# Expert blocks fed by column copies from on-chip transposed rows, addressed by token numbers in registers

## The reference

```
h = rmsnorm(x);  x += concat(sliding_window_gqa(h), multiscale_pool(h)) @ w_out
h = rmsnorm(x);  x += cross_attention(h, rmsnorm(mem)) @ xo_w          # 256 memory tokens
h = rmsnorm(x)                                                        # 512 x 2048
g_logits = h @ rg_w + rg_b                 # 4 groups; top 1
e_logits = h @ re_w[g] + re_b[g]           # 8 experts in the group; top 2, softmax of the two
for each of the 32 experts e:              # its tokens, in blocks
    y = (silu(xb @ w_gate[e]) * (xb @ w_up[e])) @ w_down[e]    # 2048 -> 512 -> 2048
    x[tokens] += gate * y
```

## Time and profile before

| | |
|---|---|
| three runs | 1660.6, 1664.76 (median), 1665.17 us |
| profiled execution | 1662.8 us, its span 1661.0 us |
| mean granted TensorE clock | 0.983 |
| PE busy | 1555.2 us (94%) |
| PE weight load busy | 887.2 us (53%) |
| DVE busy | 637.2 us (38%) |
| ACT busy | 358.0 us (22%) |
| POOL busy | 166.2 us (10%) |
| moved by DMA | 484.47 MB, mean 292 GB/s |
| chain that ended last | PE 70%, DMA 18%, DVE 7% |

### The profile page before, as it was taken

The page is one execution under the profiler, slowest core; times in us unless marked ns, Lnnn a source line. Parts: engine busy times, 40 slices in busy tenths (PEclk is TensorE's granted clock), DMA queues, the critical chain, the costliest instruction groups (busy, mean ns, idle before and its releaser), DMA issues.

```text
span 1661.0 us, 18188 instructions
## 1 busy us (share of the span) xinstructions
PE 1555.2 (94%) x7236; PEld 887.2 (53%) x7236; DVE 637.2 (38%) x783; ACT 358.0 (22%) x640; POOL 166.2 (10%) x235
## 2 busy tenths in 40 slices
PE   7999999999999999899999899889889899999997
PEld 6787777768887567733433334334334334334353
DVE  5755656652223432513322323223323223313224
ACT  6422334342223244211110011011011011101011
POOL 4470045510000000100000000000000000000000
PEclk9999999999999999999999999999999999999999
DMA  8332222353215031899999999999999999999997
GB/s 305 103 102 76 82 72 77 120 167 101 102 51 203 1 127 48 347 407 429 397 429 428 428 426 429 428 428 404 429 428 427 411 416 427 428 426 425 427 423 287
DMA packets 91773, 484.47 MB, mean 292 GB/s; under 512 B 6066, under 2 KB 44108, under 8 KB 64204
## 3 DMA queue, kind: packets, MB, share of 16 engines
q1 hardware_dynamic: 88232, 470.84, 70.0%
q0 software_dynamic: 3392, 12.92, 2.3%
q10 hardware_dynamic: 100, 0.03, 0.0%
HBM read 484.81 MB, written 8.39 MB: 297 GB/s over the span
## 4 chain that ended last, share of the span: by engine, by line
PE 70%; DMA 18%; DVE 7%; issue 2%; ACT 2%; SPq 1%; POOL 0%; DVEq 0%; POOLq 0%; ACTq 0%
PE ps L2248 22%; DMA weight_ring<-in_expert_w_up_dram 16%; PE ps L1954 10%; PE ps L1828 10%; PE ps L2274 7%; PE ps L2209 5%; PE ps L2007 3%; DVE residual L1633 3%; DMA weight_ring<-in_xkv_w_dram 1%; PE ps L1790 1%; PE ps L2070 1%; PE ps L2338 1%; PE ps L2095 1%; ACT weight_ring L898 1%; PE ps L1883 1%
## 5 line engine op out<-in xcount | busy, mean ns | idle before, releaser
L2248 PE MATMUL ps<-weight_ring,transposed_acts 128*64 128x512 f32 x2000 | 471.8, 611 | 52.6 <-DMA weight_ring<-in_expert_w_up_dram 51.3
L2248 PEld LDWEIGHTS ps<-weight_ring,transposed_acts 128*64 128x64 f32 x2000 | 158.5, 141 | 358.2 <-issue 279.5
L1633 DVE TENSOR_TENSOR residual<-ps,residual 128x1024 f32<-128x1024 f32 x128 | 150.8, 1219 | 265.3 <-PE ps L2209 264.8
L2274 PE MATMUL ps<-weight_ring,transposed_acts 128*64 128x512 f32 x960 | 212.6, 595 | 4.9 <-DVE transposed_acts L1643 4.8
L1649 DVE SCALAR_TENSOR_TENSOR y_low<-ps,proj_buffer,y_high 64x1024 fp32r<-64x1024 f32 x60 | 77.0, 1283 | 198.0 <-ACT y_high L1090 197.1
L2274 PEld LDWEIGHTS ps<-weight_ring,transposed_acts 128*64 128x64 f32 x960 | 71.9, 137 | 128.1 <-issue 125.7
L1090 ACT ACTIVATE y_high<-ps,proj_buffer 64x1024 fp32r<-64x1024 f32 x60 | 66.6, 1109 | 286.7 <-PE ps L2274 286.0
L1079 ACT ACTIVATE transposed_acts<-ps 128x512 f32<-128x512 f32 x32 | 19.1, 598 | 475.3 <-PE ps L2248 475.3
L1828 PE MATMUL ps<-mix_high,w_in_high 128*128 128x512 f32 x288 | 117.3, 407 | 1.4 <-issue 1.4
L1828 PE MATMUL ps<-normed_low,w_in_high 128*128 128x512 f32 x288 | 112.3, 390 | 0.0
L1828 PE MATMUL ps<-mix_high,w_in_low 128*128 128x512 f32 x288 | 112.3, 390 | 0.0
(11 more groups left out here) (315 smaller groups left out, 1895.3 us busy)
## 6 DMA issues: line engine op xcount, KB each, us to landing
weight_ring<-in_expert_w_down_dram SPq DMA_DIRECT2D x63, 2048.0 KB, 15.1
weight_ring<-in_expert_w_gate_dram SPq DMA_DIRECT2D x61, 2048.0 KB, 16.0
weight_ring<-in_expert_w_up_dram SPq DMA_DIRECT2D x60, 2048.0 KB, 20.3
weight_ring<-in_w_in_dram SPq DMA_DIRECT2D x18, 1024.0 KB, 5.6
weight_ring<-in_w_out_dram SPq DMA_DIRECT2D x16, 1024.0 KB, 5.0
weight_ring<-in_xkv_w_dram SPq DMA_DIRECT2D x8, 1024.0 KB, 7.6
residual<-in_x_dram SPq DMA_DIRECT2D x8, 1024.0 KB, 12.8
weight_ring<-in_xq_w_dram SPq DMA_DIRECT2D x4, 1024.0 KB, 9.8
```

Source lines behind the costliest of these rows:

```text
L1633: v.tensor_tensor(part, ps[:, bank:bank + 2, :].rearrange("p b n -> p (b n)"), part, ALU.add).then_inc(signal, 1)
L2248: ins = mm(ps[side * SLOTS:(side + 1) * SLOTS, 0, :], xsT[:, k, par * SLOTS:(par + 1) * SLOTS], gate_up_weights(e, u, kk), start=(k == 0), ...
L2274: ins = mm(ps[half, 4 + n % 2, :], act_t[:, f * SLOTS:(f + 1) * SLOTS], w[:, n * 512:(n + 1) * 512], start=(f == 0), stop=(f == KF - 1), s ...
```

## The change

The normalised rows are no longer stored and no longer gathered. H stays whole on chip, and the columns of a block are copied out of it.

- **Removed:** the buffer `normed_rows`, its four stores and ScalarE's and GpSimd's waits for them; the 17 gathers and the clearing of `hs[:, 0]` before the first; `turn_rows` and `turn_evac`; the extra buffers of expert 3, whose units 0 and 1 are now loaded through the ring like all others. SP's loop begins at expert 2.
- **Moved:** `xsT` to PB columns 0 to 2047, and the buffers `gu`, `sil`, `act_t`, `last_act_t` from H to PB. The load of `xo_w` signals on four of the ring's semaphores. The token ramp now comes behind the first column copies. `turn_gu` of a pair's second block stands before a wait for `part_added`.
- **Copies:** `copy_columns` loads 32 token numbers into registers of the engine, each with a check that it lies in 0 to 511, and issues 32 copies of 128 x 16 elements, column `where[j]` of H to a column of `xsT`, twice a block. For blocks 0 and 1 ScalarE copies slots 0 to 31 and GpSimd slots 32 to 63; in the loop GpSimd copies all 64 of each block. The copies of block b >= 2 wait until `gu_copied` has reached b - 1, that is until block b - 2 no longer needs its half of `xsT`. `gate_up` waits for the copies in place of `turn_evac`.
- **Ids:** a table `ids` (48 blocks x 64 slots, integers) is made by eight more matmuls (with the operands of the token product exchanged) and one VectorE step, and stored by GpSimd in DRAM (`block_ids`, 12 KB). The loop fetches a pair's 512 bytes with a DMA into `first_row` on one partition. For the first pair there is a path of its own: right after `ranks` VectorE makes one-hot matrices for experts 0 and 1 (`rank1`, `first_onehot`), TensorE multiplies them with the rounded token numbers (four matmuls), and VectorE writes `first_row` (`first_ids`), ahead of the rest of the router's chain. Empty slots are clamped to token 511 by `ALU.min`.
- **Logits:** the 36 router columns are now the stationary operand, and 128 tokens move; even chunks of features go to the lower half of the array, odd ones to the upper, into bank 5, which VectorE clears first. VectorE copies the result out (`logits_out`), and one more matmul with a constant matrix (`fold`) adds the two halves and turns them back to tokens on partitions (`fold_logits`). `keep_busy` counts change from 14 to 4 and 16 around the first pair's token product, and from 8 to 6 before block 0.

```diff
-            for t in range(NT):
-                pool.wait_ge(rows_ready, 4 * t + 4)
-                pool.dma_start(hn_dram[t * P:(t + 1) * P, :], hs[:, t % 2, :]).then_inc(hn_stored[t % 2], 16)
-            pool.wait_ge(hn_stored[0], 32)
-            pool.wait_ge(h_turned, 4 * 13)
-            g.memset(hs[:, 0, :], 0.0).then_inc(xs_clear, 1)
-            def gather(pair):
...
-                g.indirect_dma_start(out=xs, out_offset=None, in_=hn_dram,
-                                     in_offset=bass.IndirectOffsetOnAxis(ap=cols[:, 0:1], axis=0),
-                                     bounds_check=S - 1, oob_is_err=False).then_inc(gathered, 16)
+            def copy_columns(tokens, par, first, done, free=None):
+
+                for at in range(first, SLOTS, 32):
+                    _, where = nc.values_load_multi_w_load_instructions(
+                        tokens[:, at:at + 32], engines=(mybir.EngineType.Pool,), min_val=0, max_val=S - 1)
+                    if at == 0:
+                        pool.wait_ge(gu_copied, free)
+                    for j in range(32):
+                        ins = g.tensor_copy(xsT[:, :, par * SLOTS + at + j], H[:, :, ds(where[j], 1)].rearrange("p k n -> p (k n)"))
+                ins.then_inc(done, 1)
+
+            pool.wait_ge(first_ids, 1)
+            pool.wait_ge(h_turned, 56)
+            for par in range(2):
+                copy_columns(first_row[0:1, par * SLOTS:(par + 1) * SLOTS], par, 32, first_rows[par])
             pool.wait_ge(table_ready, 1)
             g.iota(tramp, pattern=[[1, S]], base=0, channel_multiplier=0,
                    allow_small_or_imprecise_dtypes=True).then_inc(tramp_ready, 1)
-            gather(1)
-            with pool.Fori(2, NE // 2 + 1) as it:
-                gather(it)
+            pool.wait_ge(ids_ready, 1)
+            pool.dma_start(ids_dram.rearrange("j (e s) -> (j e) s", e=2), ids[:, :]).then_inc(ids_stored, 16)
...
+            def pair_columns(it):
+                pool.dma_start(first_row[0:1, :], ids_dram[ds(it, 1), :]).then_inc(pair_ids_in, 16)
+                landed_ids = pool.to_reg(it * 16)
+                pool.wait_ge(pair_ids_in, landed_ids)
+                block_columns(it * 2, 0)
+                block_columns(it * 2 + 1, 1)
+
+            with pool.Fori(1, NE // 2) as it:
+                pair_columns(it)
@@ scalar
+            act.wait_ge(first_ids, 1)
+            act.wait_ge(h_turned, 56)
+            act.wait_ge(hT_ready, 56)
+            for par in range(2):
+                _, where = nc.values_load_multi_w_load_instructions(
+                    first_row[0:1, par * SLOTS:par * SLOTS + 32], engines=(mybir.EngineType.Activation,), min_val=0, max_val=S - 1)
+                for j in range(32):
+                    ins = a.activation(xsT[:, :, par * SLOTS + j], H[:, :, ds(where[j], 1)].rearrange("p k n -> p (k n)"), ACT.Copy)
+                ins.then_inc(first_rows[par], 1)
@@ sync
-            sp.wait_ge(hn_stored[1], 32)
-            sp.wait_ge(h_turned, 56)
-            load_extra(0)
-            sp.wait_ge(logits_done, 1)
-            load_extra(1)
-            load_extra(2)
             sp.wait_ge(table_ready, 1)
-            sp.wait_ge(gathered, 16)
...
-            load_extra(3)
...
-            with sp.Fori(EXTRA + 2, NE - 2) as b:
+            with sp.Fori(2, NE - 2) as b:
@@ vector
+            link(v.scalar_tensor_tensor(out=r["rank1"], in0=R[:, :, 0:2], scalar=1.0, in1=M_r[:, 0:NT, 0:2].bitcast(F32),
+                                        op0=ALU.add, op1=ALU.mult))
+            v.scalar_tensor_tensor(out=P_r[:, :, :], in0=wide(io[:, 0:SLOTS].unsqueeze(1), P, 2 * NT, SLOTS), scalar=1.0,
+                                   in1=wide(r["rank1"].rearrange("p t e -> p (t e)").unsqueeze(2), P, 2 * NT, SLOTS),
+                                   op0=ALU.add, op1=ALU.is_equal).then_inc(first_onehot, 1)
...
+            dve.wait_ge(first_tokens, 1)
+            v.tensor_scalar(first_row, ps[0:1, 4, 0:2 * SLOTS], float(ABSENT), float(S - 1), ALU.add, ALU.min).then_inc(first_ids, 1)
...
+            v.tensor_scalar(ids[:, :], ps[0:NBLK, 6, 0:SLOTS], float(ABSENT), float(S - 1), ALU.add, ALU.min).then_inc(ids_ready, 1)
...
-            def turn_evac(pair):
@@ tensor
-                    for k in range(4 * b, 4 * b + 4):
-                        ins = mm(ps[:, 4, t * NCOL:(t + 1) * NCOL], H[:, k, t * P:(t + 1) * P], wr[:, k, :],
-                                 start=(m == 0 and k == 4 * b), stop=(m == 3 and k == 4 * b + 3), skip_group_check=True)
+                    for j in range(4):
+                        k, side = 4 * b + j, j % 2
+                        ins = mm(ps[side * SLOTS:side * SLOTS + NCOL, 5, t * P:(t + 1) * P], wr[:, k, :], H[:, k, t * P:(t + 1) * P],
+                                 start=(m == 0 and j < 2), stop=(m == 3 and j >= 2), skip_group_check=True)
+            def fold_logits(t):
+                pe.wait_ge(halves_out, t + 1)
+                return mm(ps[:, 4, t * NCOL:(t + 1) * NCOL], LT[t % 2], fold[:, :], start=True, stop=True)
...
-            def turn_rows(pair, between=None):
...
             def gate_up(b, par, place=None, between=None):
-                if par == 0:
-                    pe.wait_ge(xsT_ready, b * 2 + 4)
+                if isinstance(b, int) and b < 2:
+                    pe.wait_ge(first_rows[b], 2)
+                else:
+                    pe.wait_ge(block_rows, b - 1)
```

More of the change, by code:

```diff
@@ L56 @@
 NSLOT = 12
-EXTRA = 3
 NA = 4
@@ L386, in hybrid_block @@
             loads_before.append(sum(1 for m in range(n) if early[m][0] == s))
-        early_loads = [sum(1 for e in early if e[0] == s) for s in range(NSLOT)]
+        before_xo = [sum(1 for e in early if e[0] == s) for s in range(NSLOT)]
+        early_loads = [n + (s in (4, 6, 8, 10)) for s, n in enumerate(before_xo)]
         def wait_past(eng, semaphore, value):
@@ L603, in _ @@
                             pattern=[[-1, P]], channel_multiplier=1).then_inc(consts, 1)
+            pool.wait_ge(consts, 2)
+            link(g.tensor_tensor(fold[:, :], ident[:, 0:NCOL], ident[:, SLOTS:SLOTS + NCOL], ALU.add))
             link(g.memset(blk[:, :], 0.0))
@@ L2148, in _ @@
             ins.then_inc(ranks, 1)
-            keep_busy(14)
+            keep_busy(4)
+            pe.wait_ge(first_onehot, 1)
+            pair_onehot = P_r[:, :, :].rearrange("p (t e) s -> p t (e s)", e=2)
+            for t in range(NT):
+                ins = mm(ps[0:2, 4, 0:2 * SLOTS], tok_r[:, t, :], pair_onehot[:, t, :], start=(t == 0), stop=(t == NT - 1))
+            ins.then_inc(first_tokens, 1)
+            keep_busy(16)
             pe.wait_ge(slot_onehot, 1)
@@ L2161, in _ @@
             ins.then_inc(gates_done, 1)
-            def turn_rows(pair, between=None):
-                rows = pair * 16 + 16
-                if not isinstance(pair, int):
-                    rows = pe.to_reg(rows)
-                pe.wait_ge(gathered, rows)
-                for q in range(4):
-                    if q == 2 and between is not None:
-                        between()
-                    for k in range(4 * q, 4 * q + 4):
-                        ins = turn(ps[:, TURN_BANKS[q], (k % 4) * P:(k % 4 + 1) * P],
-                                   hs[:, 0, k * P:(k + 1) * P], ident[:, :])
-                    ins.then_inc(xs_turned, 1)
             def expert_landed(b, u):
                 s = unit_slot(u)
-                if isinstance(b, int) and b == EXTRA and u < 2:
-                    pe.wait_ge(extra_in, 16 * 5)
-                elif isinstance(b, int) and b == 0 and u == 3:
+                if isinstance(b, int) and b == 0 and u == 3:
                     pe.wait_ge(first_up_in, 16 * 3)
```

135 lines of the change are left out of this document (61 added, 74 removed).

## The result

The changed kernel takes 1741.88 us (median of 4 runs, 1741.45 to 1744.3) beside 1663.91 us before: ratio 1.0477, 95% interval 1.0462 to 1.0492. It is 4.8% slower. Forecast were 1650 us and a range up to 1735; the forecast was wrong, and even the range misses by 7 us. The profiled execution is one of 1744.3 us with a span of 1742.5.

The account below looks back on a forecast made before the run. The weight stream was taken to set the pace, 59.4 us a pair. Gathers -20, extra buffers +9.9, start -2 and tail -0.4 gave -12.5 from 1662.8: 1650 us (chance 0.60, own range 1642 to 1658), overall range 1641 to 1735.

Parts of the forecast that it names:

- the loop: GpSimd's copies, loads and ids' DMA for a pair: 57.6 us, hidden under 59.4; 0.4 us saved in the tail.
- A second step: In the loop: GpSimd's work for a pair costs no time if it fits under the weight stream's 59.4 us.
- Rival A: GpSimd's loop, 15 pairs, sets the pace; each microsecond above 59.9 a pair costs 14.5; 1691 to 1865 us; chance 0.31.
- with one far jump a pair: Case of GpSimd setting the pace: a jump to unfetched code in its loop, a pair of 62 us, 1691 us.
- Gathers: In the weight stream: 7.9 MB of gathered rows go, 20 us saved (18.6 to 23.2).
- Extra buffers: Before block 0: four pieces of expert 3 (4.19 MB) now fall into the weight stream, 9.9 us lost.
- Start: First two blocks: ids at 689.0, first product at 702.8, 2 us earlier (bounds 6 earlier, 8 later).
- Sum without GpSimd: Whole kernel, GpSimd's loop taken as hidden: -20 + 9.9 - 2 - 0.4 = -12.5 us.
- What would show it: Signs of being wrong: TensorE waiting for copies every pair, DMA share under 0.97, pairs above 60, slow loads, first product after 708.

Follow-up runs that it names:

- e1: Changed kernel with GpSimd's 15 pairs written out instead of looped, so without the backward jump: 1682.13 us, ratio 1.0122.
- e3: Changed kernel with the ids of all 32 blocks fetched once, in one DMA before the loop; the far jump stays: 1700.43 us, ratio 1.0227.
- e4: Changed kernel without GpSimd's check of each id, run twice: 1642.05 us (ratio 0.9874), the second time 1640.7 us (0.9866).
- e2: Changed kernel with GpSimd's load-and-copy body standing once, in an inner loop over halves and blocks: 1754.62 us, ratio 1.0557.
- e5: Changed kernel without GpSimd's checks and with its 15 pairs written out instead of looped: 1661.85 us, ratio 0.9999.
- f9: Changed kernel with GpSimd's 15 pairs written out and its checks kept only on every second load of ids: 1669.83 us, ratio 1.0042.
- g13: Kernel before, with four checked loads of 32 zeros on GpSimd behind each gather, pairs written out: 1673.58 us, ratio 1.0071.
- g14: Kernel before, with four checked loads of 32 zeros on GpSimd behind each gather, in loops: 1664.51 us, ratio 1.0008.
- e6: Changed kernel with all ids fetched once and GpSimd's body standing once in an inner loop, checks kept: 1668.98 us, ratio 1.0042.
- t10: Changed kernel without GpSimd's checks, with TensorE's loop over 13 pairs written out: 1643.53 us, ratio 0.988.

## Why the prediction was wrong

**The step that failed** is the loop: "I take 6. A pair: 57.6 us. It fits, by two microseconds." GpSimd's pair takes 65.0. Term by term:

| us | forecast | measured |
|---|---|---|
| load of 32 ids | 3.6 | 2.03 |
| check, each | 0.12 | 0.23 |
| copy, each | 0.17 | 0.15 |
| half block | 12.9 | 13.2 |
| ids' DMA, issue to ids on chip | 6 | 5.8 |
| far jump | 0 | 5.2 |
| pair | 57.6 | 65.0 |

In a half the load came out 1.6 us under the forecast and the copies 0.6, the 32 checks 3.5 over it, and 1.0 of that is hidden (below): 0.3 remain, 1.3 in a pair. What decided was the jump, priced at nothing in the sum although it stood in rival A, with the earlier trace rows beside it (4.33 us for TensorE's). e1 shows its price: without it 59.5 us a pair and 60 us less. The rest (65.0 - 4 x 13.2 - 5.8 - 5.2 = 1.2) are small steps. The measured half, 13.2, is a little less than its pieces (2.03 + 32 x 0.23 + 4.8 = 14.2), because the sequencer is 1 us ahead of the copies when it begins the next load. That the sum passed the limit by so little is why the chance of 0.60 was too high.

**A second step** behind it wouldn't have held either: "That is hidden if it fits under 59.4 us". In e3 the pair takes 58.9 us and fits, and the time is 1700 us, not 1650. Theory F's kind of loss, weights that come slower where GpSimd fetches code, stands in no term of the forecast.

**Rival A** came true, in the case "with one far jump a pair". It was given 62 us a pair and 1691; at 65.0 its own formula gives 1662.8 + 5.1 x 14.5 - 2.4 = 1734. The measured profiled time is 1744. The formula left out the end. From block 2 to block 30 are 14 pairs that grow by 5.0 us, 70; and block 31's rows come 26.1 us behind block 30's, so that the stretch from block 30 to the end grows from 69.7 to 79.4, 10 more. 1662.8 + 80 = 1743.

**Gathers.** Forecast 20 us saved (18.6 to 23.2). A pair's bytes were (25.17 + 0.52) / 424 GB/s = 60.6 us in the steady stretch before and are 25.17 / 428 = 58.8 in e4: 1.8 us, 27 over 15 pairs. The mean of 59.9 that the forecast took from the earlier trace rows holds the faster first pairs. Their bytes alone would be 1.2 us a pair; that the gathers cost the rest too is read from the two rates and no run takes them out alone.

**Extra buffers.** Forecast 9.9 us lost, measured 8.0 (5 to 11). Right.

**Start.** Ids at 686.2 instead of the forecast 689.0, the first product at 700.8 instead of 702.8: the last 16 logits records took 0.56 + 0.66 instead of 1.88, and the first half on GpSimd 14.5 instead of 13.8. Within the bounds, but no term had the lower clock of the first product, which leaves 1.7 of the 4 us at its end. Block 2's rows came at 752.6, forecast 752.

**Sum without GpSimd.** Forecast -12.5, measured -22.6 in the second e4 (1663.3 to 1640.7): gathers -27 by the rates above, extras +8, which leaves -3.6 for the rest. Mechanism right, gathers sized too small. In the changed kernel the code that GpSimd fetches doesn't show, since GpSimd's pace covers it (e2 fetches none for a pair and is no faster); it decides what a half remedy brings.

**What would show it** named GpSimd's copies as what TensorE waits for, a DMA share under 0.97 and pairs above 60 as the signs of being wrong: 134.6 us, 0.94 and 65.0.

The Trainium skill (Runtime: NRT & Kernel Launch, section Instruction fetch mechanics) says that loading a register takes about 200 ns even in bulk; an estimate from that figure is 6.4 us for 32. The trace has 2.03, 63 ns each, so it doesn't hold for this load, whose source is on chip. The same section of the Trainium skill says that a taken branch out of the two fetched pages forces a fetch before the engine can go on. The traces agree: 5.2 us with a body of 50 KB, 0.83 or nothing with a small one. By the same section of the Trainium skill fetching in sequence is mostly hidden. For GpSimd's own steps that agrees (no pause in e1), and for TensorE's code too (3 us for 0.36 MB); the stream beside GpSimd's fetching doesn't agree (21 us for 0.23 MB).

## What to carry to other kernels

An engine with an idle share of 90% (GpSimd before) is no free place: add up its sequencer's steps too (loads of registers, checks, addresses, and the jump back over a long body), and compare the sum with the pace of the bound, block by block and at the last block. A sum within a few per cent of the limit doesn't tell on which side the time will fall. If ids are clamped when they are made, the check of each can go, and with it here 29 us of the engine's 65 (128 x 0.23) and the far jump.

## What was not expected of the hardware

Where GpSimd fetches more code beside a full weight stream, the stream is slower, far beyond the code's bytes. Three comparisons say so: e5 and f9 against e4, g13 against g14, e3 against e6. Above e4, by MB of code on q14 above e4's 0.17 (written out or looped alike):

| run | MB more | us more | GB/s in 855 to 1584 |
|---|---|---|---|
| e4 (second) | 0 | 0 | 428 |
| e5 | 0.23 | 21 | 420 |
| f9 | 0.35 | 29 | 415 |
| e1 | 0.49 | 41 | 411 |
| e3 | 0.71 | 60 | 401 |
| g13, above the kernel before | 0.26 | 10 | 421 (before 424) |
| t10, TensorE's q8 | 0.36 | 3 | 427 |

0.23 MB at 428 GB/s would be 0.5 us. In e1 and e3 GpSimd's slack is small as well, so their rows mix two causes; e5, f9 and g13 don't.

How the stream loses the time is not shown. Between 880 and 1580 us on the traces' clock, e5 has 77 weight packets of some 18,000 that took over twice their median (0.61 us), up to 2.6 us, the second e4 none and t10 8. But they are no mark of fetched code: the kernel before has 34, and e2, which fetches none for a pair, 177. None of e5's 77 starts within 1 us before or 3 us behind a code packet. Six of them, from 1087.0, come right behind a gap of 1.3 us from 1085.9, in which fewer than 12 packets were under way on the 16 engines, and SP issues its next weight load at 1085.91. So some are what is left when the stream had run short and starts again, and not its cause. Why GpSimd's fetching goes with a slower stream and TensorE's hardly does, and why g13 pays half of e5's price, stays open.
